# SSD scan: the decay exponents (as a Relu of the difference) and the first tap of the convolution are formed on ScalarE

## What is computed

```python
def causal_conv(x, buf, w, b):              # 4 taps
    xp = concatenate([buf, x], axis=1)
    out = xp[:, 0:L] * w[0]
    for t in range(1, 4): out = out + xp[:, t:t + L] * w[t]
    return out + b, xp[:, L:]

def step(s, inp):                           # one chunk of the scan
    xc, dtc, bc, cc = inp
    acum = cumsum(dtc * a, axis=1)
    seg = acum[:, :, None] - acum[:, None, :]
    decay = exp(where(mask, seg, -inf))     # j <= i only
    cb = einsum('bign,bjgn->bijg', cc, bc)
    y_intra = einsum('bijgh,bjghp->bighp', cb[..., None] * decay, dtc[..., None] * xc)
    y_inter = einsum('bign,bghpn->bighp', cc, s) * exp(acum)[..., None]
    w = exp(a_last[:, None] - acum) * dtc
    s_new = exp(a_last)[..., None, None] * s + einsum('bjgh,bjghp,bjgn->bghpn', w, xc, bc)
    return s_new, y_intra + y_inter
```

## Time and profile before

| | |
|---|---|
| median of 3 runs | 2334.03 us (2333.56 to 2342.25) |
| the profiled execution | 2328.8 us |
| its span, first to last instruction | 2327.3 us |
| mean granted TensorE clock | 0.955 |
| TensorE busy (products) | 2131.6 us, 92% |
| TensorE weight loads | 1983.0 us, 85% |
| VectorE busy | 1436.1 us, 62% |
| ScalarE busy | 937.9 us, 40% |
| GpSimd busy | 279.8 us, 12% |
| HBM | 183 GB/s over the span |

### The profile page before, as it was taken

The page is one execution under the profiler, slowest core; times in us unless marked ns, Lnnn a source line. Parts: engine busy times, 40 slices in busy tenths (PEclk is TensorE's granted clock), DMA queues, the critical chain, the costliest instruction groups (busy, mean ns, idle before and its releaser), DMA issues. The chain is left out here.

```text
span 2327.3 us, 41668 instructions
## 1 busy us (share of the span) xinstructions
PE 2131.6 (92%) x15171; PEld 1983.0 (85%) x15171; DVE 1436.1 (62%) x2762; ACT 937.9 (40%) x1260; POOL 279.8 (12%) x423
## 2 busy tenths in 40 slices
PE   6699999999999999968999699999999999749997
PEld 4698989999999898938999698988988988639996
DVE  5553756648465574844434468878878888744433
ACT  3444444434444334313333344544544545423332
POOL 1100201012001010120000102122121131110000
PEclk8799999999999999978999799999999999869999
DMA  4664858577658485547444466566565566336542
GB/s 126 205 174 124 276 159 276 191 226 221 210 158 284 125 281 148 190 174 269 162 156 164 133 175 194 168 194 196 168 218 182 173 200 192 102 143 220 162 154 77
DMA packets 332531, 427.42 MB, mean 184 GB/s; under 512 B 17132, under 2 KB 296220, under 8 KB 330976
## 3 DMA queue, kind: packets, MB, share of 16 engines
q1 hardware_dynamic: 293488, 287.16, 41.0%
q0 software_dynamic: 38720, 138.84, 16.8%
q10 hardware_dynamic: 224, 0.05, 0.0%
HBM read 350.63 MB, written 75.34 MB: 183 GB/s over the span
## 5 line engine op out<-in xcount | busy, mean ns | idle before, releaser
L132 DVE TENSOR_TENSOR w_lo<-w_raw,w_hi 128x1024 fp32r<-128x1024 f32 x512 | 624.9, 1225 | 651.5 <-ACT w_hi L126 641.4
L126 ACT ACTIVATE w_hi<-w_raw 128x1024 fp32r<-128x1024 f32 x512 | 541.4, 1060 | 1017.3 <-PE bank L147 950.4
L145 PE MATMUL bank<-xn_hi,w_hi 128*128 128x288 f32 x3072 | 927.9, 302 | 24.4 <-ACTq L931 12.3
L146 PE MATMUL bank<-xn_lo,w_hi 128*128 128x288 f32 x3072 | 911.7, 297 | 0.0
L147 PE MATMUL bank<-xn_hi,w_lo 128*128 128x288 f32 x3072 | 909.1, 296 | 0.0
L145 PEld LDWEIGHTS bank<-xn_hi,w_hi 128*128 128x128 f32 x3072 | 581.9, 189 | 47.5 <-issue 31.3
L146 PEld LDWEIGHTS bank<-xn_lo,w_hi 128*128 128x128 f32 x3072 | 582.7, 190 | 4.9
L147 PEld LDWEIGHTS bank<-xn_hi,w_lo 128*128 128x128 f32 x3072 | 583.3, 190 | 0.0
L145 PE MATMUL bank<-oc_o_hi,w_hi 128*128 128x288 f32 x512 | 153.9, 301 | 22.9 <-DVE oc_o_lo L1386 21.2
L145 PE MATMUL bank<-oa_o_hi,w_hi 128*128 128x288 f32 x512 | 154.5, 302 | 21.4 <-DVE oa_o_lo L1386 18.5
L146 PE MATMUL bank<-oa_o_lo,w_hi 128*128 128x288 f32 x512 | 153.8, 300 | 0.0
(11 more groups left out here) (439 smaller groups left out, 2358.1 us busy)
## 6 DMA issues: line engine op xcount, KB each, us to landing
w_raw<-in_w_in_ab SPq DMA_DIRECT2D x224, 512.0 KB, 3.9
w_raw<-in_w_in_c SPq DMA_DIRECT2D x128, 512.0 KB, 4.4
w_raw<-in_w_out_ab SPq DMA_DIRECT2D x64, 512.0 KB, 3.4
w_raw<-in_w_out_c SPq DMA_DIRECT2D x64, 512.0 KB, 3.4
state<-in_state_gla POOLq DMA_DIRECT2D x32, 512.0 KB, 10.1
out_gla_s<-state POOLq DMA_DIRECT2D x32, 512.0 KB, 4.3
state<-in_state_mlstm_c POOLq DMA_DIRECT2D x32, 512.0 KB, 9.4
out_mc_s<-state POOLq DMA_DIRECT2D x32, 512.0 KB, 4.7
```

The source lines that it names most:

```text
L126: act.activation(core.w_hi[:, j], core.w_raw[:, j % RAW], ACT.Copy).then_inc(ws["hi"], 1)
L132: dve.tensor_tensor(core.w_lo[:, j], core.w_raw[:, j % RAW], core.w_hi[:, j].bitcast(F32), ALU.subtract).then_inc(ws["split"], 1)
L145: pe.matmul(banks[m][:, 0:T], core.w_hi[:, j, kk, col], hi[:, k], start=f, stop=False)
L146: pe.matmul(banks[m][:, 0:T], core.w_hi[:, j, kk, col], lo[:, k], start=False, stop=False)
```

## The change

It does four things. The exponents of the decays are no longer formed by VectorE at steps 2 and 3 but by ScalarE, one call (two heads, eight instructions) at step 2, two at step 3 and one at step 4. They are formed as Relu(c_i - c_j) with the column as bias, positive, so the columns `pad` in `gates1` change their sign and the exponential gets a scale of -1. The first tap of the convolution goes from VectorE to ScalarE (Identity with weight as scale and bias) at step 12. ScalarE waits for the columns' copy (`cols_in`), for the taps' weights (`taps_in`) and for the broadcast of -c; VectorE waits for the first tap (`tap0`) ahead of the second.

```diff
@@ gates1, VectorE
-            dve.tensor_copy(pad[:, 0:TP], c[:, 0:TP])
-            dve.tensor_copy(pad[:, K_CS * P + 96:K_CS * P + P], c[:, S0:T])
-            dve.tensor_scalar(pad[:, K_C01 * P:K_C01 * P + P], c[:, 0:P], c[:, P - 1:P], None, ALU.subtract)
+            dve.tensor_scalar(pad[:, 0:TP], c[:, 0:TP], -1.0, None, ALU.mult)
+            dve.tensor_scalar(pad[:, K_CS * P + 96:K_CS * P + P], c[:, S0:T], -1.0, None, ALU.mult)
+            dve.tensor_scalar(pad[:, K_C01 * P:K_C01 * P + P], c[:, 0:P], -1.0, c[:, P - 1:P], ALU.mult, ALU.add)
@@ ssd_mixer, ScalarE
+        def a_args(act, q):
+
+            for h in (2 * q, 2 * q + 1):
+                for c0, c1, i0, rows, col in ((0, 128, 0, slice(0, P), K_C0), (128, 256, 128, slice(0, P), K_C01),
+                                              (256, 384, 128, slice(0, P), K_C1), (384, 416, S0, slice(96, P), K_CS)):
+                    ins = act.activation(PP[rows, h, c0:c1], nb[rows, h, i0:i0 + c1 - c0], ACT.Relu, bias=cc[rows, col, h:h + 1],
+                                         scale=-1.0)
+            ins.then_inc(s["args"], 1)
+
         def a_step(act, k, G, st):
+            if k == 2:
+                act.wait_ge(s["nb_in"], G * 16 + 16)
+                act.wait_ge(s["cols_in"], G + 1)
...
                 act.activation(turned[b % 4], bk[:, :], ACT.Copy).then_inc(free[at(f"st{b}", 0)[0]], 1)
+            if k in (2, 3, 4):
+                for q in ((0,), (1, 2), (3,))[k - 2]:
+                    a_args(act, q)
             if k in (5, 6):
                 for q in ((0, 1), (2, 3))[k - 5]:
                     act.wait_ge(s["args"], G * 4 + (q + 1))
-                    act.activation(PP[:, 2 * q:2 * q + 2], PP[:, 2 * q:2 * q + 2], ACT.Exp).then_inc(s["exps"], 1)
+                    act.activation(PP[:, 2 * q:2 * q + 2], PP[:, 2 * q:2 * q + 2], ACT.Exp, scale=-1.0).then_inc(s["exps"], 1)
...
         def a_prep(act, k, gg, st):
+            if k == 12:
+                act.wait_ge(s["taps_in"], gg + 1)
+                act.wait_ge(s["proj_free"], gg * SL + 3)
+                for m in range(6):
+                    ins = act.activation(cy[:, m, 0:CL], xp[:, m, 0:CL], ACT.Identity, scale=cw[:, m, 0:1], bias=cw[:, m, 4:5])
+                ins.then_inc(s["tap0"], 1)
@@ ssd_mixer, VectorE
-                st.then_wait(ins)
+                ins.then_inc(s["taps_in"], 1)
+                dve.wait_ge(s["taps_in"], gg + 1)
...
-            if 12 <= k <= 15:
+            if 13 <= k <= 15:
                 tap = k - 12
+                if tap == 1:
+                    dve.wait_ge(s["tap0"], gg + 1)
                 for m in range(6):
                     w_ = cw[:, m, tap:tap + 1]
-                    if tap == 0:
-                        ins = dve.tensor_scalar(cy[:, m, 0:CL], xp[:, m, 0:CL], w_, cw[:, m, 4:5], ALU.mult, ALU.add)
-                    else:
-                        ins = dve.scalar_tensor_tensor(cy[:, m, 0:CL], xp[:, m, tap:tap + CL], w_, cy[:, m, 0:CL], ALU.mult, ALU.add)
+                    ins = dve.scalar_tensor_tensor(cy[:, m, 0:CL], xp[:, m, tap:tap + CL], w_, cy[:, m, 0:CL], ALU.mult, ALU.add)
...
-        def v_args(dve, q):
-
-            for h in (2 * q, 2 * q + 1):
-                for c0, c1, i0, rows, col in ((0, 128, 0, slice(0, P), K_C0), (128, 256, 128, slice(0, P), K_C01),
-                                              (256, 384, 128, slice(0, P), K_C1), (384, 416, S0, slice(96, P), K_CS)):
-                    ins = dve.tensor_scalar(PP[rows, h, c0:c1], nb[rows, h, i0:i0 + c1 - c0], cc[rows, col, h:h + 1], 0.0,
-                                            ALU.add, ALU.min)
-            ins.then_inc(s["args"], 1)
-
...
-                dve.tensor_copy(cc[:], g["cols"][:, :, bass.ds(G * 8, 8)])
+                dve.tensor_copy(cc[:], g["cols"][:, :, bass.ds(G * 8, 8)]).then_inc(s["cols_in"], 1)
...
-            if k in (2, 3):
-                if k == 2:
-                    dve.wait_ge(s["nb_in"], G * 16 + 16)
-                v_args(dve, 2 * k - 4)
-                v_args(dve, 2 * k - 3)
```

More of the change, by code:

```diff
@@ L1551, in ssd_mixer @@
                                  "st_used brow xsd tanh_z zg gated squared o_ready o_stored r_first pst_out pst_stored "
-                                 "tails tail_out upd dve act pool_w").split()}
+                                 "tails tail_out upd dve act pool_w cols_in taps_in tap0").split()}
         b_arrived = [sem(f"b_arrived{j}") for j in range(RAW)]
```

## The result

The changed kernel takes 2,356.85 us in the median of 5 runs, the kernel before 2,335.36: a ratio of 1.0088 with a 95% interval of 1.0067 to 1.0109. Run again beside the experiments it takes 2,358.26, a ratio of 1.0114 (1.0098 to 1.0130). It is slower by about 1%, 20 to 25 us, and above the forecast range of 2,328 to 2,352. One execution of 2,710.70 us, with a mean granted clock of 0.824, stands outside the comparison; the lines of after come from the same kernel profiled beside the experiments (2,357.25 us).

What follows compares the result with a forecast made beforehand. TensorE was taken to bound the second mixer, VectorE next. At a = 2.3, +4.9 (six steady turns) + 2.1 (first scanned group) - 0.7 (last turn) = +6.3 us on 2,334.0, giving 2,340.3; range 2,328 to 2,352.

Steps and rivals of the forecast that it cites:

- What bounds the mixer: In full turns of the second mixer TensorE, busy 85.0 of 89 us, bounds; VectorE's exponents are covered seven times of eight.
- Where the calls hurt: ScalarE's late split of step 5 delays the fourth update product: 0.8 us in six turns, 2.1 in the first scanned group.
- the formula 3a - 6.1: New wait of TensorE's fourth update product per steady turn, a being one call's us on ScalarE; zero up to 2.03.
- a sign of being wrong: Inter-group products waiting for the fourth evacuation, moved waits at L2087 or L2070, or a shorter turn would refute the prediction.
- The price of a call: One call of eight instructions on ScalarE: a taken as 2.3 us, with bounds of 1.1 and 3.0.
- the overlap of neighbours: On ScalarE, two neighbouring exponentials in 1.68 us overlap by 0.09 us; the same was taken for the short instructions.
- the case of dear calls: Rival: a of 2.6 to 3.0 us makes the split of step 5 late; 2,347.5 to 2,357 us; chance 0.15.
- The clock: Rival: TensorE falls to half clock behind L2087 in none or all seven turns; -4.5 to +6 us on any case.
- The last turn: Without projection, exponents leaving VectorE gain 7.6 - 3a = 0.7 us, passing through to L2087.
- the chain that was forecast to be late next: Last turn: inter-group products after three calls and three evacuations, then an update product and updates 2 and 3, 2,030.8 + 3a.
- The first tap: Step 12: 2.18 us off VectorE worth nothing; 3.4 us on ScalarE covered by a 5.62 us gap.
- Function tables: Rival: Relu or Identity wants another table than Exp, loads of 1.28 us; 10 more, 2,351 us; chance 0.04.

## Why the prediction was wrong

- **What bounds the mixer**: right. TensorE does; the waits at L2087 and L2070 kept their length (17.6 and 8.3 us), and none of VectorE's 7.6 us a group came back in a full turn.
- **Where the calls hurt**: right, place and size, once the price of a call is put right. With the measured a = 2.67 the formula 3a - 6.1 gives 1.9 us a turn; the waits are 0.62 + 1.19, 2.15 us from start to start. That the inter-group products wait for the fourth evacuation was named as a sign of being wrong, and it came. It follows from the price: the prediction put its threshold at a = 2.5, and 2a + 1,491.7 = 1,497.0 against 1,496.65 gives 0.4 us, 0.6 measured. Splitting the calls up, dropping the operand and reordering VectorE each took away what they should.
- **The price of a call**: the step that failed. 2.3 us was taken, 2.67 is measured, and every 0.1 us is worth 2.4: 9 of the 16.5 us by which the forecast of 2,340.3 fell short. The parts: the duration was right without the operand (296 estimated, 301 measured at 128 columns), and so was the operand, 0.1 us as VectorE's (97 and 90 ns measured). Wrong was the overlap of neighbours: 0.09 us, taken from exponentials of 832 columns. Eight instructions of 398 and 316 ns add up to 3.02 us and take 2.67, 0.05 us of overlap each. The upper bound, 3.0 with no overlap at all, held. What came is the case of dear calls (a of 2.6 to 3.0), which had a chance of 0.15.
- **The clock**: the second step that failed. The rival was named, with -4.5 to +6 us on top of any case, and came out beyond its end: seven turns with a fall instead of three, about 7.5 us more. The bounds took 1.5 us for each fall; the turns of before already show one of 3.0, and after has two. It was given too little room in the range: at a = 2.67 the sum is 2,334.0 + 15 = 2,349, inside it, and the clock's 7.5 make 2,356.5 against the 2,356.85 that were measured. That these two add up so well is in part luck: the median of before alone moved by 1.3 us when two executions were added.
- **The last turn**: 0.4 us lost by the formula at a = 2.67; the inter-group rows stand 38.9 us behind the first transposes instead of 38.0, and the product at L1809 51.8 instead of 51.4. The inter-group products wait 5.25 us there for the fourth evacuation, the chain that was forecast to be late next.
- **The first tap**: right, 3.32 us on ScalarE and no effect. **Function tables**: no new load, 19 at each of L163 and L164 in both kernels; Relu and Identity ran with the table that was in place.

Open is why the clock falls in one turn and not in its neighbour with the same order of work, and so how a change shifts the number of falls.

## What to carry to other kernels

An engine with half its time free is no free engine: what counts is the room in front of its next piece of work that others wait for, here 6.1 us for three calls that took 8.0 (4.7 us of idle time on ScalarE itself, 1.2 in which update 0 had stood behind VectorE's own exponents, and 0.25 until TensorE came to the product). Price many short instructions by neighbours of the same length; an overlap read from long ones was too good here (0.09 us taken, 0.05 measured). A late split or evacuation carries its delay over to whatever is queued behind it on another engine: moving update 0 ahead of VectorE's half of the split gave back 8.9 us here, with ScalarE as late as before.

## What the runs showed of the hardware

- An activation of 128 columns takes 301 ns with constant operands and 398 with one per-partition operand, 226 and 316 at 32 columns; 312 columns with two such operands take 633. The Trainium skill (ScalarE: Activation LUTs, What ACT_TABLE_LOAD costs) gives about 93 ns for each pointer operand, and the trace agrees (97 and 90). It also lets neighbours overlap by about 93 ns; six taps of 312 columns do (six of 633 ns in 3.32 us), but eight exponents of 128 and 32 columns overlap by only 50.
- TensorE's half clock (granted 0.50) repeats: behind the same wait of 1.96 us, with turns otherwise alike, some runs of turns stay at full clock (89.16 us each) and others fall in every turn. With the tap alone on ScalarE five turns in a row took 92.2 us, 3.0 of it half clock (two of them):

```profile
1655.00:1747.00 92.00, 87.84 (x643) 81.53 (x642) 72.11 (x173) 45.35 (x70) 18.10 (x27) 0.96 0.60 183
1747.00:1839.00 92.00, 87.84 (x644) 81.54 (x643) 71.94 (x173) 45.34 (x70) 18.12 (x27) 0.96 0.60 184
```

The many executions of the kernel before spread from 2,326.0 to 2,348.4 us; the six of the kernel before with the wait taken away from 2,310.1 to 2,314.8, the twelve of the changed kernel with it taken away from 2,326.2 to 2,333.7. That the falls of the clock make the difference in spread is likely, not shown.
